# Second operand buffer stored in rows of 272 elements, and transposed probabilities of the first keys placed in the angle table

## The chip, the cores and the metric

The kernel runs on one NeuronCore of a Trainium2 chip. The metric is the device time of one execution in microseconds, the median of several runs. Everything is float32 in memory. The matrix products are made on TensorE from operands that are split in a high and a low part.

## What is computed

Two transformer blocks, one after the other, on one sequence of 256 tokens with 2048 features. The first puts 16 learned tokens in front, so it works on 272.

```python
def reference(x, meta, ...):
    x = first_block(...)      # h = [meta, x]
                              # h += mixer(rmsnorm(h)) @ w_out    attention with a forget gate, and a short convolution
                              # h += (silu(h @ w_gate) * (h @ w_up)) @ w_down
                              # rmsnorm(h)[:, 16:]
    return second_block(x, ...)
                              # q, k, v, u, gates = x @ w_in ; rope ; dilated attention ; pooling
                              # merged @ w_out ; layer_norm
                              # f = square(relu(x @ w_ff1)) @ w_ff2 ; layer_norm(ALPHA * x + f)
```

## The kernel before, in words

Features lie on the 128 partitions and tokens along the free dimension, so a product takes a 128x128 weight tile as the stationary operand and a strip of up to 512 columns of activations as the moving operand. All weights stream from memory once, in units of 128 partitions by 1024 elements (4096 bytes per partition): two contraction tiles (kt) of four output tiles (x). SyncE loads units into `raw` (5 slots), ScalarE rounds each into `w_hi` (L812) and VectorE subtracts it to get `w_lo` (L1203), both with 4 slots. A plan, `make_plan`, writes out the steps: a block of four output tiles runs over all its units, and in each unit over its four tiles. All engines walk the same list of steps and meet in semaphores.

The activations that TensorE reads stand in two buffers, `a_op` and `b_op`. Each has for every contraction tile kt two rows, the high part (index 0) and the low part (index 1):

```python
a_op = sb("a_op", [P, KT, 2, TOK], F32R)        # TOK = 272
b_op = sb("b_op", [P, KT, 2, SEQ + 2], F32R)    # SEQ + 2 = 258
```

So in `a_op` a row has 1088 bytes per partition, and in `b_op` 1032. Stages that read `a_op`: k, q, v, conv, gu (gate and up of the first feed-forward), k2, q2, v2, u, gate, out2, ff2. Stages that read `b_op`: out, down, ba, bp, ff1. Stages alternate so that one buffer is filled while the other is read. `a_op` is read from element 16 on in the stages that leave the 16 learned tokens out; `b_op` from element 0.

In most stages ("pair" columns) `product_step` reads both rows in one instruction, as a pattern of 2 rows by 256 elements. For the even kt of a unit it issues L578, w_hi times both rows (512 columns), and L579, w_lo times the high row (256 columns); for the odd kt L581, w_lo times the high row, and L582, w_hi times both rows. These four instructions are called a quad here: 1536 columns of moving data. There are 1984 quads on `a_op` and 992 on `b_op`: 128 in out, 64 in group 0 of down and 96 in each of its groups 1 to 3, 128 in ba and bp, and 128 in each of groups 1 to 3 of ff1. Group 0 of ff1 ("affine" columns) takes two more columns, the 257th and 258th element of each row, which hold the gain and the bias of the layer norm, and makes three products of 258 columns (L585, L586, L587). The stages k, v and most of conv are also made of such threes.

`b_op` is written by ScalarE (high rows: L905, L942, L973, L1053, L1068, L1085) and VectorE (low rows: L1368, L1427, L1525, L1634, L1660, L1726).

`probs_t2` is used in the attention of the first block alone: eight times, once a head, ScalarE copies the transposed probabilities of keys 256 to 271 into it (L882, 16 partitions by 128 elements) and TensorE reads it (L677). `turn_tab` (512 elements a partition) holds, in its first 272 elements on 8 partitions, the running sum of the forget gates (`csum`, L1294, read at L1296 and L638, all by 88 us), and from 484 us on the tables of sines and cosines of the rotary embedding (`sinr` in elements 256 to 511, `cosr` in 0 to 255).

Buffers are laid out in SBUF in the order of their declaration: `h`, `a_op`, `b_op`, `raw`, `w_hi`, `w_lo`, `q`, `k`, `v`, `ytile`, `probs`, `probs_t`, `probs_t2`, then constants and work buffers. They fill all but about 1.4 KB of a partition.

Of the kernel before, what the change touches and what calls it, by code (L numbers as in the profile page):

```python
# [8 lines left out]
F32R = mybir.dt.float32r  # L9
# [5 lines left out]
P = 128  # L15
D = 2048
KT = D // P
SEQ = 256
META = 16
TOK = META + SEQ  # L20
# [161 lines left out]
def two_blocks(nc, w, tokens, params, consts, mask1, mask2, positions, out):  # L182
# [5 lines left out]
    with ExitStack() as ctx:  # L188
        def sb(name, shape, dt=F32):
            return ctx.enter_context(nc.sbuf_tensor(name, shape, dt))  # L190
# [4 lines left out]

        h = sb("h", [P, KT, TOK])
        a_op = sb("a_op", [P, KT, 2, TOK], F32R)
        b_op = sb("b_op", [P, KT, 2, SEQ + 2], F32R)
        raw = sb("raw", [P, RAW, UNIT])
        w_hi = sb("w_hi", [P, SPLIT, UNIT], F32R)  # L200
        w_lo = sb("w_lo", [P, SPLIT, UNIT], F32R)
# [3 lines left out]
        ytile = sb("ytile", [P, KT, SEQ])  # L205
        probs = sb("probs", [P, 2, SEQ + TOK])
        probs_t = sb("probs_t", [P, 2 * SEQ])
        probs_t2 = sb("probs_t2", [META, P])
        con = sb("con", [P, N_CONST])
        masks = sb("masks", [P, 2 * (P + SEQ)])  # L210
        par = sb("par", [P, N_PARAMS])
# [1 line left out]
        row = sb("row", [P, TOK])  # L213
        shift = sb("shift", [P, SEQ])
        turn_tab = sb("turn_tab", [P, 2 * SEQ])
        cosr, sinr = turn_tab[:, 0:SEQ], turn_tab[:, SEQ:2 * SEQ]
        acc = sb("acc", [P, TOK])
        acc2 = sb("acc2", [P, SEQ])
# [1837 lines left out]
```

## Time and profile before

| | |
|---|---|
| median of 3 runs | 2489.11 us (2488.93 to 2490.05) |
| the profiled execution's own time | 2489.91 us |
| its span, first to last instruction | 2488.1 us |
| TensorE busy with matmuls | 2451.6 us, 99% of the span |
| weight loads on TensorE (beside the matmuls) | 2170.8 us, 87% |
| VectorE, ScalarE, GpSimd busy | 1616.2, 1193.4, 217.2 us (65, 48, 9%) |
| granted TensorE clock, mean | 0.996 of full |
| DMA | 449.60 MB, mean 181 GB/s; the weight queue's packets take 57.0% of 16 engines' span |

The profiled execution took 0.80 us more than the median, and 1.8 us of its time lie outside its span. Durations of matmuls overlap in the profile: an instruction of 512 columns is shown as 390 to 400 ns long while the next one starts about 230 ns after it. What a stage costs is therefore read from the starts of its instructions.

### The profile page before, as it was taken

The numbers are of one execution on the slowest core, as the hardware profiler recorded it, in microseconds if no ns is written. First come the engines' busy times: TensorE is split into PE (matmuls) and PEld (weight loads), VectorE is DVE, ScalarE is ACT, GpSimd is POOL, SyncE is SP. The second block draws the span as 40 slices with busy tenths as digits, with TensorE's granted clock in tenths as the row PEclk, the third lists the DMA queues.
The fourth block names the chain that finished last, engine by engine and source line by source line (L and its number), as shares of the span: only waits on it lengthen the run. The fifth ranks groups of instructions, "written<-read, shape, count | busy, mean of one in ns | idle before, by whom it ended". The sixth has DMA issues, their size and how long they took to land.

```text
span 2488.1 us, 36373 instructions
## 1 busy us (share of the span) xinstructions
PE 2451.6 (99%) x14746; PEld 2170.8 (87%) x14746; DVE 1616.2 (65%) x2466; ACT 1193.4 (48%) x1724; POOL 217.2 (9%) x231
## 2 busy tenths in 40 slices
PE   8999999999999999999999999999999999999997
PEld 8898888888888888888888888888998888888885
DVE  5645577766666665667676756677885665565667
ACT  6444445544444443455554544555454443443544
POOL 0001111000000000001220202033200000000022
PEclk9999999999999999999999999999999999999998
DMA  7554445566665656656555465565565666666563
GB/s 246 171 159 128 124 155 181 183 198 189 191 188 179 196 192 187 187 186 201 186 185 154 143 212 190 182 195 183 162 198 187 187 188 190 188 189 191 181 193 102
DMA packets 125752, 449.60 MB, mean 181 GB/s; under 512 B 13840, under 2 KB 16400, under 8 KB 125584
## 3 DMA queue, kind: packets, MB, share of 16 engines
q1 hardware_dynamic: 125296, 446.91, 57.0%
q8 instruction: 116, 1.90, 0.3%
q14 instruction: 52, 0.43, 0.0%
q10 hardware_dynamic: 288, 0.36, 0.0%
HBM read 445.12 MB, written 2.10 MB: 180 GB/s over the span
## 4 chain that ended last, share of the span: by engine, by line
PE 94%; DVE 3%; ACT 1%; issue 1%; DMA 0%; SPq 0%; POOL 0%; ACTq 0%; DVEq 0%
PE out_bank L582 27%; PE out_bank L578 27%; PE out_bank L581 14%; PE out_bank L579 14%; PE out_bank L585 3%; PE out_bank L586 3%; PE out_bank L587 3%; DVE w_lo L1203 1%; ACT w_hi L812 1%; DMA raw<-in_w_in 0%; PE side_bank L657 0%; PE side_bank L656 0%; PE side_bank L695 0%; PE out_bank L604 0%; PE side_bank L679 0%
## 5 line engine op out<-in xcount | busy, mean ns | idle before, releaser
L1203 DVE TENSOR_TENSOR w_lo<-raw,w_hi 128x1024 fp32r<-128x1024 f32 x839 | 1039.8, 1242 | 634.7 <-ACT w_hi L812 631.5
L812 ACT CAST w_hi<-raw 128x1024 fp32r<-128x1024 f32 x840 | 876.6, 1048 | 958.6 <-PE out_bank L582 873.2
L582 PE MATMUL out_bank<-a_op,w_hi 128*128 128x512 f32 x1984 | 785.1, 396 | 0.0
L578 PE MATMUL out_bank<-a_op,w_hi 128*128 128x512 f32 x1984 | 781.6, 394 | 1.5 <-DVE w_lo L1203 0.8
L581 PE MATMUL out_bank<-a_op,w_lo 128*128 128x256 f32 x1984 | 557.6, 281 | 0.0
L579 PE MATMUL out_bank<-a_op,w_lo 128*128 128x256 f32 x1984 | 550.1, 277 | 0.0
L579 PEld LDWEIGHTS out_bank<-a_op,w_lo 128*128 128x128 f32 x1984 | 372.6, 188 | 83.0
L581 PEld LDWEIGHTS out_bank<-a_op,w_lo 128*128 128x128 f32 x1984 | 371.8, 187 | 83.2
L582 PE MATMUL out_bank<-b_op,w_hi 128*128 128x512 f32 x992 | 392.0, 395 | 0.0
L578 PE MATMUL out_bank<-b_op,w_hi 128*128 128x512 f32 x992 | 391.6, 395 | 0.0
L578 PEld LDWEIGHTS out_bank<-a_op,w_hi 128*128 128x128 f32 x1984 | 373.8, 188 | 4.6 <-DVE w_lo L1203 2.4
L582 PEld LDWEIGHTS out_bank<-a_op,w_hi 128*128 128x128 f32 x1984 | 372.8, 188 | 0.0
L579 PE MATMUL out_bank<-b_op,w_lo 128*128 128x256 f32 x992 | 278.4, 281 | 0.0
L581 PE MATMUL out_bank<-b_op,w_lo 128*128 128x256 f32 x992 | 277.5, 280 | 0.0
L581 PEld LDWEIGHTS out_bank<-b_op,w_lo 128*128 128x128 f32 x992 | 187.7, 189 | 43.5
L579 PEld LDWEIGHTS out_bank<-b_op,w_lo 128*128 128x128 f32 x992 | 186.9, 188 | 44.4
L582 PEld LDWEIGHTS out_bank<-b_op,w_hi 128*128 128x128 f32 x992 | 186.8, 188 | 0.0
L578 PEld LDWEIGHTS out_bank<-b_op,w_hi 128*128 128x128 f32 x992 | 186.7, 188 | 0.0
L1220 DVE TENSOR_TENSOR work<-work,out_bank 128x256 f32<-128x256 f32 x248 | 102.5, 416 | 118.6 <-ACT work L831 117.8
L585 PE MATMUL out_bank<-a_op,w_hi 128*128 128x258 f32 (+1 forms) x504 | 147.4, 292 | 0.1
L586 PE MATMUL out_bank<-a_op,w_hi 128*128 128x258 f32 (+1 forms) x504 | 144.5, 287 | 0.0
L587 PE MATMUL out_bank<-a_op,w_lo 128*128 128x258 f32 (+1 forms) x504 | 144.0, 286 | 0.0
(285 smaller groups left out, 1998.0 us busy)
## 6 DMA issues: line engine op xcount, KB each, us to landing
raw<-in_w_ff SPq DMA_DIRECT2D x256, 512.0 KB, 4.2
raw<-in_w_in SPq DMA_DIRECT2D x223, 512.0 KB, 3.7
raw<-in_w_gu SPq DMA_DIRECT2D x176, 512.0 KB, 4.2
raw<-in_w_down SPq DMA_DIRECT2D x88, 512.0 KB, 4.2
raw<-in_w_out SPq DMA_DIRECT2D x64, 512.0 KB, 4.3
raw<-in_w_ba SPq DMA_DIRECT2D x16, 512.0 KB, 4.2
raw<-in_w_bp SPq DMA_DIRECT2D x16, 512.0 KB, 4.1
out<-h SPq DMA_DIRECT2D x8, 256.0 KB, 2.1
```

Source lines behind the costliest of these rows:

```text
L578: t_.e.matmul(bank[:, :], wh, a_both, start=start, stop=False, skip_group_check=True)
L579: mm = t_.e.matmul(bank[:, 0:SEQ], wl, a_hi, start=False, stop=stop, skip_group_check=True)
L581: t_.e.matmul(bank[:, 0:SEQ], wl, a_hi, start=False, stop=False, skip_group_check=True)
L582: mm = t_.e.matmul(bank[:, :], wh, a_both, start=False, stop=stop, skip_group_check=True)
L585: t_.e.matmul(to, wh, a_hi, start=start, stop=False, skip_group_check=True)
L586: t_.e.matmul(to, wh, a_lo, start=False, stop=False, skip_group_check=True)
L587: mm = t_.e.matmul(to, wl, a_hi, start=False, stop=stop, skip_group_check=True)
L812: a.e.copy(w_hi[:, m % SPLIT, :], raw[:, u % RAW, :]).then_inc(hi_split)
L1203: v_.e.tensor_tensor(w_lo[:, m % SPLIT, :], raw[:, u % RAW, :], w_hi[:, m % SPLIT, :].bitcast(F32), ALU.subtract).then_inc(lo_split)
L1220: v_.e.tensor_tensor(y, y, bank_of(tile)[:, 0:SEQ], ALU.add).then_inc(bank_free)
```

## The change

`b_op` gets rows of 272 elements, so that a row has 1088 bytes and a contraction tile 2176, as in `a_op`; before it was 1032 and 2064. Nothing is written to or read from the elements added, and every instruction takes the same numbers of elements as before. That costs 1792 bytes more per partition. `probs_t2` is no longer a buffer (512 bytes less): it is elements 272 to 399 of `turn_tab` on 16 partitions, behind `csum` and inside the later `sinr`.

```diff
-        b_op = sb("b_op", [P, KT, 2, SEQ + 2], F32R)
+        b_op = sb("b_op", [P, KT, 2, TOK], F32R)
...
-        probs_t2 = sb("probs_t2", [META, P])
...
         turn_tab = sb("turn_tab", [P, 2 * SEQ])
+        probs_t2 = turn_tab[0:META, TOK:TOK + P]
         cosr, sinr = turn_tab[:, 0:SEQ], turn_tab[:, SEQ:2 * SEQ]
```

No engine's list of instructions changes, but for the name of the tile in the 8 copies at L882 and the 8 matmuls at L677. The addresses: `h` and `a_op` stay (`a_op` at 33920, `b_op` at 68736), `raw` to `probs_t` move up by 1792 bytes (`raw` from 101760 to 103552, `w_hi` from 122240 to 124032), and everything from `con` on by 1280. In bytes from a multiple of 64, the start of the high row in `b_op` was 16 x kt and of the low row 16 x kt + 8 (modulo 64); it is now 0 for every row, as in `a_op`.

## Rows read from the trace of the kernel before

**Rows 1.** The page's busy times and the chain that ended last.
```profile
span 2488.1 us, 36373 instructions
PE 2451.6 (99%) x14746; PEld 2170.8 (87%) x14746; DVE 1616.2 (65%) x2466; ACT 1193.4 (48%) x1724; POOL 217.2 (9%) x231
...
PE 94%; DVE 3%; ACT 1%; issue 1%; DMA 0%; SPq 0%; POOL 0%; ACTq 0%; DVEq 0%
```

**Rows 2.** Stretches of gu 3, down 3, ff1 2, ff2 2: busy time (instructions), clock, DMA.
```profile
core 0: us, PE busy (x) PEld busy (x) DVE busy (x) ACT busy (x) POOL busy (x), PEclk, DMA share, GB/s
...
980.00:1113.00 133.00, 133.00 (x769) 116.45 (x768) 81.62 (x117) 63.96 (x91) 0.00 (x0) 1.00 0.61 190
1113.00:1180.00 67.00, 67.00 (x384) 58.48 (x383) 50.16 (x73) 36.45 (x56) 10.40 (x11) 1.00 0.60 193
...
2109.00:2198.00 89.00, 89.00 (x510) 77.71 (x509) 53.00 (x75) 42.07 (x58) 0.00 (x0) 1.00 0.62 187
2199.00:2287.00 88.00, 88.00 (x510) 77.05 (x509) 51.94 (x69) 34.81 (x36) 0.00 (x0) 1.00 0.61 190
```

**Rows 3.** Line L578 by stage on `a_op` (gu 1, gu 3, gate 1, ff2 1): count, duration min/median/max, first and last start.
```profile
L578 PE MATMUL out_bank<-a_op,w_hi x192: 388/390/390, 579.2 to 711.6; 128*128 128x512 f32 x192
L578 PE MATMUL out_bank<-a_op,w_hi x192: 390/390/397, 980.0 to 1112.4; 128*128 128x512 f32 x192
L578 PE MATMUL out_bank<-a_op,w_hi x128: 390/390/400, 1519.9 to 1607.9; 128*128 128x512 f32 x128
L578 PE MATMUL out_bank<-a_op,w_hi x128: 390/390/400, 2020.1 to 2108.2; 128*128 128x512 f32 x128
```

**Rows 4.** Line L578 by stage on `b_op` (down 0, down 1, down 3, ba/bp, ff1 1).
```profile
L578 PE MATMUL out_bank<-b_op,w_hi x64: 387/392/397, 534.5 to 578.5; 128*128 128x512 f32 x64
L578 PE MATMUL out_bank<-b_op,w_hi x96: 387/394/405, 712.3 to 778.9; 128*128 128x512 f32 x96
L578 PE MATMUL out_bank<-b_op,w_hi x96: 387/394/405, 1113.1 to 1179.7; 128*128 128x512 f32 x96
L578 PE MATMUL out_bank<-b_op,w_hi x64: 387/394/405, 1475.0 to 1519.2; 128*128 128x512 f32 x64
L578 PE MATMUL out_bank<-b_op,w_hi x128: 387/394/405, 1930.3 to 2019.4; 128*128 128x512 f32 x128
```

**Rows 5.** Timeline of TensorE in ff1 2: the starts of kt 10, 12, 14 and the next kt 0.
```profile
2122.85 0.40 PE L578 MATMUL out_bank<-b_op,w_hi 128*128 128x512 f32 x1
...
2125.66 0.39 PE L578 MATMUL out_bank<-b_op,w_hi 128*128 128x512 f32 x1
...
2128.43 0.40 PE L578 MATMUL out_bank<-b_op,w_hi 128*128 128x512 f32 x1
...
2131.27 0.40 PE L578 MATMUL out_bank<-b_op,w_hi 128*128 128x512 f32 x1
```

**Rows 6.** Line L578 on `a_op` in q2 and in ff2 0.
```profile
L578 PE MATMUL out_bank<-a_op,w_hi x64: 388/394/399, 1226.0 to 1270.1; 128*128 128x512 f32 x64
L578 PE MATMUL out_bank<-a_op,w_hi x128: 388/390/399, 1840.7 to 1929.6; 128*128 128x512 f32 x128
```

**Rows 7.** Groups of the products of 258 columns on both buffers: busy us, mean ns | idle before.
```profile
L585 PE MATMUL out_bank<-a_op,w_hi 128*128 128x258 f32 x256 | 75.4, 294 | 0.0
L586 PE MATMUL out_bank<-a_op,w_hi 128*128 128x258 f32 x256 | 73.1, 285 | 0.0
L586 PE MATMUL out_bank<-b_op,w_hi 128*128 128x258 f32 x256 | 72.9, 285 | 0.0
L585 PE MATMUL out_bank<-b_op,w_hi 128*128 128x258 f32 x256 | 72.8, 284 | 0.2 <-DVE w_lo L1203 0.2
```

**Rows 8.** Groups of VectorE that write low rows, and the copy and product of `probs_t2` (shown as probs_t).
```profile
L1641 DVE TENSOR_TENSOR a_op<-work,a_op 128x256 fp32r<-128x256 f32 x64 | 25.8, 422 | 0.0
L1427 DVE TENSOR_TENSOR b_op<-work,b_op 128x256 fp32r<-128x256 f32 x44 | 18.4, 419 | 0.0
...
L882 ACT COPY probs_t<-side_bank x8: 249/254/256, 175.2 to 294.1; 16x128 f32<-16x128 f32 x8
```

## Prediction

> **What bounds the kernel now.** I read the page's busy times and its chain first: TensorE is busy with matmuls 99% of the span and holds 94% of the chain that ended last, while the other engines stand at 65, 48 and 9% [rows 1]. Then the busy time in four stretches of the long feed-forward stages: TensorE is busy for the whole of each, at full clock, with VectorE at about 60% and the DMA engines at 0.61 [rows 2]. So nothing feeds TensorE too slowly there. What sets the end is the pace at which TensorE itself goes from one matmul to the next, and only an edit that changes that pace, or makes it wait, can show.
>
> The durations of matmuls don't tell the pace, since they overlap. The starts do. Line L578 starts once in each quad (1536 columns of moving data), so the time from the first to the last start of a stage, over the count less one, is the time of a quad:
>
> - On `a_op` [rows 3]: gu 1 and gu 3 take 132.4 us / 191 = 693.2 ns, gate 1 takes 88.0 / 127 = 692.9 ns, ff2 1 takes 88.1 / 127 = 693.7 ns. Call it 693.3.
> - On `b_op` [rows 4]: down 1 and down 3 take 66.6 / 95 = 701.1 ns, ba and bp 44.2 / 63 = 701.6 ns, ff1 1 takes 89.1 / 127 = 701.6 ns, down 0 takes 44.0 / 63 = 698.4 ns.
>
> The same four instructions with the same widths and the same weight tiles are thus about 8 ns slower a quad when the moving operand comes from `b_op`. Nothing waits in either kind of stage. What differs is where the rows begin. In `a_op` every row begins at a multiple of 64 bytes, and the time is the same in whichever stage. In `b_op` the start moves by 16 bytes with each kt and by 8 more for the low row, and the time moves with it. In ff1 2 the four quads of kt 12 and 13 take 2128.43 - 2125.66 = 2.77 us (693 each), those of kt 10 and 11 take 2.81 us (703) and those of kt 14 and 15 take 2.84 us (710) [rows 5]. A buffer whose pace depends on kt, by up to 17 ns, while the instructions are the same, points to the address of the operand. That is the edit's lever.
>
> **The change part by part.**
>
> *Rows of 272 in `b_op`, the pair products.* No instruction is added, removed or moved. I price 992 quads at the pace of `a_op`, 693.3: 288 in down 1 to 3 x 7.8 ns = 2.2 us; 384 in ff1 1 to 3 x 8.3 = 3.2 us; 128 in ba and bp x 8.3 = 1.1 us; 64 in down 0 x 5.1 = 0.3 us; and 128 in out, a stage with other work between, taken at the same 8.3 as an estimate, 1.1 us. Sum 7.9 us. All of it lies on TensorE's path, at full weight.
>
> `a_op` has a second pace, though. In q2 and in ff2 0 a quad takes 44.1 / 63 and 88.9 / 127 = 700.0 ns, the same instructions from the same aligned rows [rows 6]. There L578 is shown with durations from 388 to 399 ns, where gu 1 has 388 to 390. So aligned rows don't give 693.3 for certain: TensorE has two patterns and can stay in either for a whole stage. If `b_op` takes the slow one, the gain is 288 x 1.1 + 512 x 1.6 + 128 x 1.6 = 1.3 us, less 64 x 1.6 = 0.1 for down 0: 1.2 us. These are the bounds of this term: 1.2 and 7.9 us. Of the `a_op` stages that have little else on TensorE (gu 1 to 3, gate 1, ff2 1 and 2 with 960 quads, against q2 and ff2 0 with 192) five sixths run at the fast pace. Weighted so, the gain is 5/6 x 7.9 + 1/6 x 1.2 = 6.8 us. I take this value.
>
> What limits the trust in it: the high row of `b_op` will begin at 0 modulo 128 and the low row at 64, while `a_op` without its 16 learned tokens has it the other way round (64, then 0). No stage of before runs pairs in that arrangement.
>
> A low row of `b_op` begins 8 bytes past a multiple of 16 now, for every kt alike, and a high row at a multiple of 16. If only those 8 bytes mattered, the price would be the same at each kt, and rows 5 show that it isn't; what they would cost is rival C below. The Trainium skill (SBUF — State Buffer, "Door 1: The DMA port swizzle", the note on SBUF cachelines) says that SBUF has lines of 16 bytes and that each access that crosses to a new line pays a penalty. By that rule it would be just these 8 bytes that cost: 65 lines a low row where aligned ones have 64.
>
> *The products of 258 columns in ff1 0.* Their groups on `b_op` are no slower than on `a_op`: 285 against 285 ns at L586, 284 against 294 at L585 [rows 7]. I take zero, bounded by half the quads' difference, as each such three has half the columns: 256 threes x 4.2 ns = 1.1 us either way.
>
> *Writes to the low rows.* VectorE takes 419 ns into `b_op` and 422 into `a_op` [rows 8]: nothing to gain, and VectorE has room.
>
> *`probs_t2` in `turn_tab`.* Eight copies of 254 ns on ScalarE [rows 8] and eight small products keep their form and place. `csum` and `probs_t2` don't overlap, the sines are written some 180 us after the last of these copies. Zero.
>
> *Everything from `raw` on moved by 1792 bytes.* The distance between the moving operand and the weights changes. But in before this distance already changes with each unit (4352 bytes of operand against 4096 of weights) and the quads of gu 1 stay within 388 to 390 ns in duration and at 693.2 in pace [rows 3]. So I take zero. If the distance did matter, the bound is that of the slow pattern, below.
>
> *What is late next.* With 8 ns less per quad nothing new binds: in gu the same chain of split and load serves the faster pace, without a gap [rows 2].
>
> **Sum.** The profiled execution took 2489.91 us, 0.80 more than the median; I forecast medians. 2489.91 - 0.80 - 6.8 = 2482.3 us.
>
> **The rivals.**
>
> *A: aligned rows alone don't help.* `b_op` settles in the slow pattern, or the arrangement 0/64 is not as good as 64/0, or the pace hangs on something other than the row's start. For it: q2 and ff2 0 at 700.0 ns on rows that all begin at a multiple of 64 [rows 6]. Against: kt 12 reaches 693 with its high row on a multiple of 64, and the dependence on kt. Gain between 0 and 2 us, 2487 to 2489 us.
>
> *B: slower, because the pattern is inherited.* In before, gu 1, gu 3, gate 1 and ff2 1 come straight after a stage on `b_op`, and run fast; q2 and ff2 0 come after k2 (on `a_op`) and after the threes of ff1 0, and run slow. Perhaps the irregular rows of `b_op` shake TensorE out of the slow pattern each time, and once all rows are aligned nothing does: the slow one, once entered, lasts over the stages. Then 960 quads on `a_op` lose 700.0 - 693.3 = 6.7 ns each, 6.4 us, against the 1.2 us that `b_op` still gains: 5.2 us slower, 2494.3 us. It decides once more than 180 of the 960 quads change over (180 x 6.7 = 1.2 us) with `b_op` in the slow pattern too. For it: both patterns last for whole stages. Against: the side work of attention and norms, and each change of buffer, disturb TensorE as well.
>
> *C: only the 8 bytes of the low rows cost.* Each quad reads a low row twice (L578, L582), and a fetch of 4 elements more at 693.3 / 1536 = 0.451 ns a column costs 1.8 ns; 1984 such reads make 3.6 us, 2485.5 us. For it: `b_op` is slower on average by a few ns. Against: kt 12 runs at 693 with the same 8 bytes, and kt 14 at 710 [rows 5]. This is what the cachelines note of the Trainium skill would make of the change; no stage here has a pair with low rows alone shifted.
>
> *D: more than forecast.* All of `b_op` at 693.3 (7.9 us) and the stages now slow turned fast as well: 192 quads in q2 and ff2 0 x 6.7 = 1.3 us, and perhaps 1.5 us in stages that mix both. 10.7 us, 2478.4 us.
>
> **How the numbers follow.** Measuring this kernel can tell 0.2%, 5.0 us, from no change: faster is under 2484.1, slower over 2494.1. Forecast (2480 to 2485 us) 0.42, D 0.08, A 0.32, B 0.08, C 0.06, something not thought of 0.04 (half of it slower). Faster: the forecast's and D's, less a small part of the forecast that ends above 2484.1: 0.47. Slower: 0.08 (part of B stops short of the bound). Same: 0.45. The range has to take in the forecast and A, which with C hold 8 in 10: 2479.5 to 2489.5 us, and with some room for the stages of `a_op` that may change pattern, to 2490. The forecast's own range is 2480 to 2485.
>
> **What would show it.** Right: the starts of L578 in down, ff1, ba and bp give 693 to 696 ns a quad; kt 12 and kt 14 take the same time in ff1 2; the longest duration of L578 on `b_op` falls from 405 to 400 ns or less; gu, gate 1 and ff2 1 stay at 693. A: `b_op` at 700, with durations of L578 up to 399. B: gu or ff2 1 at 700. Wrong altogether if TensorE gains idle time before L578 or if VectorE's writes into `b_op` change by more than some ns.

## The result and the profile after

The changed kernel takes 2495.14 us (median of 10 runs, 2492.68 to 2496.45), the kernel before 2490.28 us in the same comparison (2488.93 to 2492.47). The ratio is 1.0019, 95% interval 1.0011 to 1.0027: 4.9 us slower, against a forecast of 6.8 us faster. The profiled execution took 2496.45 us with a span of 2494.6 us.

The page's busy times and chain, to hold against [rows 1]:

```profile
span 2494.6 us, 36373 instructions
PE 2457.9 (99%) x14746; PEld 2174.6 (87%) x14746; DVE 1615.8 (65%) x2466; ACT 1193.4 (48%) x1724; POOL 217.2 (9%) x231
...
PE 94%; DVE 3%; ACT 1%; issue 1%; DMA 0%; SPq 0%; ACTq 0%; DVEq 0%
```

The same engine bounds the kernel, the other engines did the same work in the same time, and TensorE is busy 6.3 us longer. Its pace by stage, line L578 on `b_op` in down 1, down 3, ba/bp, ff1 1 and ff1 2, to hold against [rows 4] (count, duration min/median/max in ns, first and last start in us):

```profile
L578 PE MATMUL out_bank<-b_op,w_hi x96: 390/398/398, 714.9 to 782.0; 128*128 128x512 f32 x96
L578 PE MATMUL out_bank<-b_op,w_hi x96: 391/398/398, 1116.8 to 1183.9; 128*128 128x512 f32 x96
L578 PE MATMUL out_bank<-b_op,w_hi x64: 390/398/398, 1479.8 to 1524.3; 128*128 128x512 f32 x64
L578 PE MATMUL out_bank<-b_op,w_hi x128: 390/397/398, 1934.9 to 2024.6; 128*128 128x512 f32 x128
L578 PE MATMUL out_bank<-b_op,w_hi x128: 390/397/398, 2114.0 to 2203.8; 128*128 128x512 f32 x128
```

A quad now takes 67.1 / 95 = 706.3, 44.5 / 63 = 706.3 and 89.7 / 127 = 706.3 ns, where before it took 701. The expectations below write 706.7, the pace within a stage: the first unit of a stage, with quads of about 700, is not in it. Neither pace of `a_op` (693.3 and 700.0) has appeared on `b_op`, but a third one. The dependence on kt is gone, as forecast. Four starts of line L578 in ff1 2, for kt 10, 12, 14 and the next kt 0, to hold against [rows 5]:

```profile
2128.14 0.40 PE L578 MATMUL out_bank<-b_op,w_hi 128*128 128x512 f32 x1
...
2130.97 0.40 PE L578 MATMUL out_bank<-b_op,w_hi 128*128 128x512 f32 x1
...
2133.80 0.40 PE L578 MATMUL out_bank<-b_op,w_hi 128*128 128x512 f32 x1
...
2136.62 0.40 PE L578 MATMUL out_bank<-b_op,w_hi 128*128 128x512 f32 x1
```

A unit (four output tiles, so four quads) takes 2.82 or 2.83 us, where before the units took 2.77 to 2.84. Aligned rows made the pace even, at a worse level. On `a_op` (gu 3, q2, ff2 0), to hold against [rows 3] and [rows 6]:

```profile
L578 PE MATMUL out_bank<-a_op,w_hi x192: 390/390/392, 983.7 to 1116.1; 128*128 128x512 f32 x192
L578 PE MATMUL out_bank<-a_op,w_hi x64: 390/390/391, 1230.1 to 1273.8; 128*128 128x512 f32 x64
L578 PE MATMUL out_bank<-a_op,w_hi x128: 389/390/400, 1846.1 to 1934.2; 128*128 128x512 f32 x128
```

gu 3 stays at 132.4 / 191 = 693.2 ns, and q2 and ff2 0 went from 700.0 to the fast pace (43.7 / 63 and 88.1 / 127, 693.7 ns). So the change costs 992 x 5.3 = 5.3 us on `b_op`, and 192 quads of `a_op` take 1.2 us less: 0.8 in ff2 0 and 0.4 in q2. The 0.4 us can't be put down to the new rows, since q2 is fast with the old ones too (old_rows below). That makes 4.1 of the 4.9 us. The spans of the two profiled executions differ by 6.5 us, because in the one of after TensorE's granted clock was lower in q and in u. Stretches 61 to 90, 90 to 112, 1316 to 1376 and 86 to 91 us, before and then after (the number ahead of the DMA share is the mean granted clock):

```profile
61.00:90.00 29.00, 26.27 (x156) 22.74 (x155) 18.97 (x40) 16.78 (x25) 0.00 (x0) 1.00 0.47 146
90.00:112.00 22.00, 22.00 (x131) 19.36 (x130) 12.13 (x15) 9.52 (x13) 0.00 (x0) 1.00 0.63 191
1316.00:1376.00 60.00, 58.01 (x339) 50.13 (x338) 45.23 (x102) 28.92 (x47) 9.57 (x16) 1.00 0.50 154
...
86.00:91.00 5.00, 3.28 (x19) 2.91 (x20) 4.83 (x11) 1.39 (x3) 0.00 (x0) 1.00 0.23 51
```

```profile
61.00:90.00 29.00, 26.27 (x150) 22.67 (x149) 19.11 (x39) 16.54 (x25) 0.00 (x0) 0.97 0.48 146
90.00:112.00 22.00, 22.00 (x122) 19.27 (x121) 10.41 (x13) 8.38 (x10) 0.00 (x0) 0.96 0.60 188
1316.00:1376.00 60.00, 58.14 (x331) 50.38 (x330) 42.51 (x95) 28.99 (x48) 6.61 (x12) 0.97 0.49 151
...
86.00:91.00 5.00, 3.45 (x14) 3.00 (x15) 4.83 (x11) 1.39 (x3) 0.00 (x0) 0.73 0.22 66
```

In q the fall stands at a pause of TensorE, which is busy for 3.3 to 3.5 of these 5 us in both executions; the kernel before kept its full clock through it. Such a dip is not tied to the new rows: the profiled execution of old_rows has 0.97 and 0.96 in the first two of these stretches, and 1.00 in the third. The dips cost 3.0 us here, 1.7 in q and 1.3 in u, by the starts of line L578.

### The profile page after: what moved, and what is told of

Read it like the earlier page. It is cut to its first block, busy times and chain, and to the rows that moved or that the text cites. A ratio compares the mean times of both kernels' runs of the same rounds, so it can differ in the third digit from the quotient of the medians.

```text
span 2494.6 us, 36373 instructions
## 1 busy us (share of the span) xinstructions
PE 2457.9 (99%) x14746; PEld 2174.6 (87%) x14746; DVE 1615.8 (65%) x2466; ACT 1193.4 (48%) x1724; POOL 217.2 (9%) x231
## 4 chain that ended last, share of the span: by engine, by line
PE 94%; DVE 3%; ACT 1%; issue 1%; DMA 0%; SPq 0%; ACTq 0%; DVEq 0%
PE out_bank L578 27%; PE out_bank L582 27%; PE out_bank L581 14%; PE out_bank L579 14%; PE out_bank L585 3%; PE out_bank L586 3%; PE out_bank L587 3%; DVE w_lo L1203 1%; ACT w_hi L812 0%; DMA raw<-in_w_in 0%; PE side_bank L657 0%; PE side_bank L656 0%; PE side_bank L695 0%; PE out_bank L604 0%; PE side_bank L679 0%
## 5 line engine op out<-in xcount | busy, mean ns | idle before, releaser
L582 PE MATMUL out_bank<-a_op,w_hi 128*128 128x512 f32 x1984 | 787.2, 397 | 0.0
L578 PE MATMUL out_bank<-a_op,w_hi 128*128 128x512 f32 x1984 | 782.6, 394 | 1.6 <-DVE w_lo L1203 0.9
L578 PE MATMUL out_bank<-b_op,w_hi 128*128 128x512 f32 x992 | 394.4, 398 | 0.0
L582 PE MATMUL out_bank<-b_op,w_hi 128*128 128x512 f32 x992 | 389.9, 393 | 0.0
L578 PEld LDWEIGHTS out_bank<-a_op,w_hi 128*128 128x128 f32 x1984 | 374.2, 189 | 4.6 <-DVE w_lo L1203 2.5
L582 PEld LDWEIGHTS out_bank<-a_op,w_hi 128*128 128x128 f32 x1984 | 373.3, 188 | 0.0
L579 PE MATMUL out_bank<-b_op,w_lo 128*128 128x256 f32 x992 | 282.5, 285 | 0.0
L581 PE MATMUL out_bank<-b_op,w_lo 128*128 128x256 f32 x992 | 279.8, 282 | 0.0
L582 PEld LDWEIGHTS out_bank<-b_op,w_hi 128*128 128x128 f32 x992 | 187.5, 189 | 0.0
L578 PEld LDWEIGHTS out_bank<-b_op,w_hi 128*128 128x128 f32 x992 | 186.3, 188 | 0.0
L585 PE MATMUL out_bank<-a_op,w_hi 128*128 128x258 f32 (+1 forms) x504 | 147.5, 293 | 0.6 <-DVE a_op L1208 0.5
L586 PE MATMUL out_bank<-a_op,w_hi 128*128 128x258 f32 (+1 forms) x504 | 144.5, 287 | 0.0
```

What stands on the lines that cost most here:

```text
L578: t_.e.matmul(bank[:, :], wh, a_both, start=start, stop=False, skip_group_check=True)
L579: mm = t_.e.matmul(bank[:, 0:SEQ], wl, a_hi, start=False, stop=stop, skip_group_check=True)
L581: t_.e.matmul(bank[:, 0:SEQ], wl, a_hi, start=False, stop=False, skip_group_check=True)
L582: mm = t_.e.matmul(bank[:, :], wh, a_both, start=False, stop=stop, skip_group_check=True)
L585: t_.e.matmul(to, wh, a_hi, start=start, stop=False, skip_group_check=True)
L586: t_.e.matmul(to, wh, a_lo, start=False, stop=False, skip_group_check=True)
```

## Experiments

The theory after the result was that the pace depends on where the rows of the moving operand begin modulo 128 (theory P). The first rivals were that it depends on their place relative to the weights (R), or on something other than addresses (Q). In all kernels below each instruction is as in the changed one, but for the two nudges; only places in SBUF differ. Each diff is against the changed kernel, and that of before_w_128 against the kernel before. Each kernel has one profiled execution, so a pace of a stage is read from one execution, while the times are medians of 2 to 11. For reference, with places modulo 256 and the weights' start taken off: the high row at an even kt stands at 64 in `a_op`, before and after, and at 0 in `b_op` after. This is called rel from the second set on. At odd kt it is 128 more.

**Old rows in the new places** (label old_rows)

```diff
-        b_op = sb("b_op", [P, KT, 2, TOK], F32R)
+        b_op = sb("b_op", [P, KT, 2, SEQ + 2], F32R); pad1 = sb("pad1", [P, KT * 28])
```

> The changed kernel with b_op back in rows of 258 elements and 1792 bytes of padding behind it, so that every other buffer stands exactly where the change put it, probs_t2 inside turn_tab too. If the rows of b_op are the whole cause: b_op back at about 701 ns a quad, 5.3 us less than the changed kernel, the time of before (2490). If the moved buffers or the place of probs_t2 cost something by themselves: it stays above before by that, up to 2495.

Measured: 2489.82 us, ratio to before 0.9999 (0.9989 to 1.0008). Line L578 in gu 3, down 3, q2 and ff2 0:

```profile
L578 PE MATMUL out_bank<-a_op,w_hi x192: 390/390/397, 981.7 to 1114.2; 128*128 128x512 f32 x192
L578 PE MATMUL out_bank<-b_op,w_hi x96: 387/394/405, 1114.9 to 1181.4; 128*128 128x512 f32 x96
L578 PE MATMUL out_bank<-a_op,w_hi x64: 390/390/390, 1227.7 to 1271.3; 128*128 128x512 f32 x64
L578 PE MATMUL out_bank<-a_op,w_hi x128: 388/390/399, 1841.7 to 1930.6; 128*128 128x512 f32 x128
```

`b_op` is back at 66.5 / 95 = 700 ns with the scattered durations of before. The loss comes from the rows of `b_op`. The moved buffers, and `probs_t2` in `turn_tab`, cost nothing that the interval of 0.1% would show. ff2 0 is back at 88.9 / 127 = 700.0 ns as well, but q2 is not: it takes 43.6 us for 63 quads, the fast pace, where before it took 44.1, though all that TensorE reads there has the same places modulo 256 and the same widths. So a stage can change from one pace to the other without any of these edits.

**`b_op` 64 bytes further** (label b_at_64)

```diff
+        pad0 = sb("pad0", [P, 16])
         b_op = sb("b_op", [P, KT, 2, TOK], F32R)
+        pad1 = sb("pad1", [P, 16])
```

> The changed kernel with 64 bytes of padding ahead of b_op and 64 behind it: high rows of b_op begin at 64 modulo 128 and low rows at 0, as the rows of a_op do in the pair stages; everything else stays where it is modulo 128. Theory P (the pace is set by where the moving rows begin modulo 128, and 64 then 0 is the good order, 0 then 64 the bad one): quads on b_op go from 706.7 to 693.3 ns, 992 x 13.4 ns = 13.3 us less than the changed kernel (about 2482), so 8 us less than before. Rival Q (the stages on b_op are slower for another reason, such as the engines that write or the stage's own waits): 706.7 stays, 2495. Theory P but with the slow pattern of q2 in some stages: 693 to 700, 2482 to 2488.

Measured: 2497.78 us, ratio 1.0025 (1.0015 to 1.0034). A miss for P and for Q. gu 3 and down 3:

```profile
L578 PE MATMUL out_bank<-a_op,w_hi x192: 392/394/395, 985.2 to 1118.9; 128*128 128x512 f32 x192
L578 PE MATMUL out_bank<-b_op,w_hi x96: 392/394/395, 1119.6 to 1186.1; 128*128 128x512 f32 x96
```

`b_op` did get better, 66.5 / 95 = 700.0 ns, but `a_op`, which was not touched, went from 693.3 to 133.7 / 191 = 700.0. What had moved for `a_op` was the weights, by 128 bytes.

**Only what lies behind `b_op` 64 bytes further, and only the split weights** (labels weights_at_64, only_w_64)

```diff
         b_op = sb("b_op", [P, KT, 2, TOK], F32R)
+        pad1 = sb("pad1", [P, 16])                       # weights_at_64
...
+        pad0 = sb("pad0", [P, 16])                       # only_w_64
         w_hi = sb("w_hi", [P, SPLIT, UNIT], F32R)
         w_lo = sb("w_lo", [P, SPLIT, UNIT], F32R)
+        pad1 = sb("pad1", [P, 16])                       # only_w_64
```

> The changed kernel with 64 bytes of padding behind b_op only: a_op and b_op stay, the weights (raw, w_hi, w_lo) and all behind them now begin at 64 modulo 128. Theory P (place of the moving rows alone): nothing changes, a_op at 693.3 and b_op at 706.7 ns a quad, 2495 us. Rival R (the place of the moving rows relative to the weights counts, both being read at once): the roles swap, a_op goes to 706.7 (1984 x 13.4 = 26.6 us more) and b_op to 693.3 (13.3 us less), 2508 us.

> The changed kernel with 64 bytes between raw and w_hi and 64 behind w_lo: only the split weights, which TensorE loads, stand 64 bytes further modulo 128; raw, the work buffers and all others keep their places. If the pace hangs on the moving rows against the loaded weights: as in weights_at_64, a_op at 706.7 (rel 0) and b_op at 700.0 (rel 192), near 2507 us. If on another buffer that moved along in weights_at_64 (raw, the work buffers): as the changed kernel, 693.3 and 706.7, 2495 us.

Measured: 2507.41 us (ratio 1.0065, 1.0047 to 1.0084) and 2506.65 us (1.0067, 1.0044 to 1.0090). gu 3 and down 3 in weights_at_64:

```profile
L578 PE MATMUL out_bank<-a_op,w_hi x192: 390/397/398, 986.1 to 1121.1; 128*128 128x512 f32 x192
L578 PE MATMUL out_bank<-b_op,w_hi x96: 392/394/400, 1121.8 to 1188.3; 128*128 128x512 f32 x96
```

and in only_w_64:

```profile
L578 PE MATMUL out_bank<-a_op,w_hi x192: 390/397/398, 986.0 to 1121.0; 128*128 128x512 f32 x192
L578 PE MATMUL out_bank<-b_op,w_hi x96: 392/394/400, 1121.7 to 1188.2; 128*128 128x512 f32 x96
```

Neither operand moved, and the paces changed on both: `a_op` to 135.0 / 191 = 706.8 ns, `b_op` to 700.0. P is out. The second run leaves `raw` in place, and the work buffers at their places modulo 128 (they move by 128, where weights_at_64 moved them by 64), and does the same, so it is the place of the moving rows against the weights that TensorE loads that counts. R had `b_op` at 693.3; it is 700.0, at rel 192 where `a_op` used to have rel 64.

**`b_op` and the weights moved together** (label both_at_64)

```diff
+        pad0 = sb("pad0", [P, 16])
         b_op = sb("b_op", [P, KT, 2, TOK], F32R)
```

> The changed kernel with 64 bytes of padding ahead of b_op only: b_op and the weights both begin at 64 modulo 128, a_op stays. Theory P: a_op 693.3, b_op 693.3, about 2482 us. Rival R (relative place): b_op keeps 706.7 since it moved along with the weights, and a_op goes to 706.7 as well, 2495 + 26.6 = 2522 us.

Measured: 2515.57 us, ratio 1.0098 (1.0080 to 1.0116). gu 3 and down 3:

```profile
L578 PE MATMUL out_bank<-a_op,w_hi x192: 397/397/398, 990.1 to 1125.0; 128*128 128x512 f32 x192
L578 PE MATMUL out_bank<-b_op,w_hi x96: 397/397/398, 1125.7 to 1192.9; 128*128 128x512 f32 x96
```

As R says: `b_op` keeps its bad pace when it moves along with the weights, and `a_op` gets it too. The forecast of 2522 was too high: it took 13.4 ns more for each of 1984 quads. The 1152 quads of gu 1 to 3, q2, gate 1 and ff2 0 to 2 did lose 13.3, and gu 0 12.3, but k2 and ff2 3 lost 8.2, out2 7.6, v2 5.8 and group 0 of gate 3.1, where the quad in the middle took 704 ns already.

**`b_op` at rel 64 with the weights kept modulo 256** (label b_at_64_w_kept)

```diff
+        pad0 = sb("pad0", [P, 16])
         b_op = sb("b_op", [P, KT, 2, TOK], F32R)
+        tiny = sb("tiny", [P, 3, 16])
...
-        tiny = sb("tiny", [P, 3, 16])
```

> The changed kernel with 64 bytes ahead of b_op and the small buffer tiny moved behind it (192 bytes), so that the weights move by 256 in all. Write rel for the start of the high row at an even kt less the start of the weights, modulo 256. The runs so far had rel 64 (a_op before and after: mostly 693.3 ns a quad), rel 0 (b_op of the changed kernel, both buffers of both_at_64, a_op of weights_at_64: 706.7) and rel 192 (both buffers of b_at_64, b_op of weights_at_64: 700.0). Here both buffers have rel 64. Theory G (rel alone sets the pace): 693.3 on both, 992 x 13.4 = 13.3 us less than the changed kernel, about 2482. Rival H (with all rows alike the slow pattern is entered and kept, which is why b_at_64 ran at 700.0 everywhere): 700.0 on both, like b_at_64, about 2497. Between: some stages at each.

Measured: 2486.98 us, ratio 0.9987 (0.9978 to 0.9996), the first layout that beats the kernel before. gu 3, down 3, ff1 2 and ff2 2:

```profile
L578 PE MATMUL out_bank<-a_op,w_hi x192: 390/390/390, 977.5 to 1110.0; 128*128 128x512 f32 x192
L578 PE MATMUL out_bank<-b_op,w_hi x96: 390/390/390, 1110.7 to 1176.5; 128*128 128x512 f32 x96
L578 PE MATMUL out_bank<-b_op,w_hi x128: 388/394/399, 2106.9 to 2195.8; 128*128 128x512 f32 x128
L578 PE MATMUL out_bank<-a_op,w_hi x128: 388/394/399, 2196.5 to 2285.4; 128*128 128x512 f32 x128
```

Both G and H are half right. In gu 1 to 3 and in down all quads run at 693, `b_op` included (65.8 / 95 = 693). From ba on, behind the stages with much other work on TensorE, ba, bp, gate 1, ff2 0 to 2 and ff1 1 to 3 all run at 88.9 / 127 = 700.0, `a_op` included, which before ran fast in gate 1 and ff2 2. So rel 64 has two patterns. The pace from the starts tells them apart; durations do so less surely (388/390/399 in ff2 0 of before is slow, 389/390/400 in ff2 0 of after is fast).

The starts also show where TensorE changes from one to the other. In ff2 3 of this kernel, the quads ahead of two small products of the layer norm and those behind them:

```profile
L578 PE MATMUL out_bank<-a_op,w_hi x40: 388/394/399, 2375.7 to 2403.0; 128*128 128x512 f32 x40
...
2404.44 0.59 PE L735 MATMUL side_bank<-acc,ones 128*128 128x256 f32 x2
...
L578 PE MATMUL out_bank<-a_op,w_hi x57: 390/390/390, 2409.7 to 2448.6; 128*128 128x512 f32 x57
```

They take 27.3 / 39 = 700 and 38.9 / 56 = 695 ns (693.4 by the starts to the hundredth of a us). In the profiles of the seven kernels with `a_op` at rel 64 no two neighbouring units on `a_op` that ran at the paces 693 and 700 differed in it: between a fast unit and a slow one there always stands a unit lengthened by something else, or another stage. q2 takes over the pace at which k2 ends, 700 in before and 693 in old_rows.

**`b_op` at rel 128** (label b_at_128_w_kept) and **the kernel before with the weights 128 bytes further** (label before_w_128)

```diff
+        pad0 = sb("pad0", [P, 32])                                # b_at_128_w_kept
         b_op = sb("b_op", [P, KT, 2, TOK], F32R)
+        gms = sb("gms", [P, KT, 2])                               # and taken out below
...
         b_op = sb("b_op", [P, KT, 2, SEQ + 2], F32R)
+        pad1 = sb("pad1", [P, 32])                                # before_w_128
```

> As the run beside it, but with 128 bytes ahead of b_op and gms behind it: b_op has rel 128, a_op keeps rel 64. Not seen so far. Theory G: b_op takes some fixed pace of its own; since even and odd kt merely change roles between rel 0 and rel 128, 706.7 is the guess (2495 us), 693 to 700 possible (2482 to 2489). a_op stays at 693.3 in gu 1 to 3 by both theories.

> The kernel before with 128 bytes behind b_op: its irregular rows of 258 stay, but a_op gets rel 192 where it had 64. Theory G: a_op goes from 693.3 to 700.0 in gu 1 to 3, gate 1 and ff2 1 and 2: 960 x 6.7 = 6.4 us more than before, about 2496. Rival H (irregular rows shake TensorE into the fast pattern, whatever rel is): a_op stays at 693.3 in these stages, 2490.

Measured: 2495.35 us (ratio 1.0022, 1.0012 to 1.0032) and 2500.34 us (1.0037, 1.0023 to 1.0052). gu 3 and down 3 of b_at_128_w_kept:

```profile
L578 PE MATMUL out_bank<-a_op,w_hi x192: 390/390/399, 981.8 to 1114.3; 128*128 128x512 f32 x192
L578 PE MATMUL out_bank<-b_op,w_hi x96: 392/395/397, 1115.0 to 1182.1; 128*128 128x512 f32 x96
```

and gu 3 and ff2 2 of before_w_128:

```profile
L578 PE MATMUL out_bank<-a_op,w_hi x192: 392/394/400, 984.8 to 1118.5; 128*128 128x512 f32 x192
L578 PE MATMUL out_bank<-a_op,w_hi x128: 392/394/395, 2208.8 to 2297.7; 128*128 128x512 f32 x128
```

Rel 128 gives 67.1 / 95 = 706.3 ns, as guessed. In before_w_128 `a_op` runs at 700.0 with rel 192 although `b_op` keeps its irregular rows: at rel 192 no fast pattern was seen, with irregular rows or without. The stages of the estimate lost 6.3 us, as forecast. The time rose by 9.7 us: gu 0, out2, ff2 3, k2 and v2 lost 1.7 us more, and the stages on `b_op`, whose rows had moved against the weights as well, about 0.8 us. For the rest, 0.9 us, no stage is known.

**Other places** (labels rel_32, rel_96), as b_at_64_w_kept, with `pad1` of 8 elements behind `tiny`, or `ln_tiny` and 16 elements in place of `tiny`.

> b_at_64_w_kept with the weights 32 bytes further, so that both buffers have rel 32. Not seen with rows all alike; in the kernel before, quads at kt 2 (high row at rel 32, the odd kt's 16 bytes beyond) took 699 ns. If the pace falls in steps of 6.7 ns between 0 (706.7) and 64 (693.3 or 700.0): 700.0, near 2495. The quads of before were never under 691, so no gain is expected.

> The same with the weights 32 bytes nearer, both buffers at rel 96. In the kernel before kt 6 took 705 and kt 14 took 710 ns. If that belongs to the place of the high row: 706.7 or more on both, 2976 quads x 13.4 ns above 693.3, about 2520 us.

Measured: 2515.25 us (ratio 1.0098, 1.0080 to 1.0117) and 2498.63 us (1.0031, 1.0019 to 1.0044). gu 3, first rel_32, then rel_96:

```profile
L578 PE MATMUL out_bank<-a_op,w_hi x192: 397/397/397, 988.8 to 1123.8; 128*128 128x512 f32 x192
```

```profile
L578 PE MATMUL out_bank<-a_op,w_hi x192: 395/395/395, 984.0 to 1117.7; 128*128 128x512 f32 x192
```

Both guesses missed, rel_32 to the slow side and rel_96 to the fast, and for one reason: I carried the paces of kt 2, 6 and 14 over from the kernel before, where the low row and the odd kt stand elsewhere. Rel 32 is as bad as 0, and 96 as 192.

| rel of the high row, even kt | ns a quad | seen on |
|---|---|---|
| 0 | 706 to 707 | `b_op` after; both buffers in both_at_64; `a_op` in weights_at_64, only_w_64 |
| 32 | 707 | both in rel_32 |
| 64 | 693.3 or 700.0 | `a_op` before and after; both in b_at_64_w_kept |
| 96 | 700.0 | both in rel_96 |
| 128 | 706 | `b_op` in b_at_128_w_kept |
| 192 | 700.0 | both in b_at_64; `b_op` in weights_at_64, only_w_64; `a_op` in before_w_128 |

Rel 0 and rel 192 were each seen with the weights at two different places modulo 256, and had the same pace at both.

**A nudge at the start of a stage** (labels nudge_shifted, nudge_plain). On top of b_at_64_w_kept, 17 matmuls more, each written to a bank and overwritten there by the product that follows:

```diff
+                        if start and tile is first_tile[blk.stage, blk.group] and blk in late:
+                            t_.e.matmul(bank[:, 0:240], wh, a_hi[:, 16:256], start=True, stop=True, skip_group_check=True)
```

with `late` the blocks of pair columns from ba on; nudge_plain reads `a_hi[:, 0:240]`.

> b_at_64_w_kept with one matmul of 240 columns more at the start of 17 stages from ba on, written to the stage's first bank and overwritten by the product that follows; its moving operand begins 64 bytes later, at rel 128. Theory H+ (rel 64 has two patterns; a stage keeps the one it is in, and reading once from rows in the arrangement 0/128 throws TensorE into the fast one, as down, ba, bp and ff1 do for the stages behind them in the changed kernel): the stages from ba to ff1 3, some 1024 quads at 700.0, go to 693.3: 6.9 us less, 17 x 0.12 = 2.0 us more, 2482 us. Rival: one matmul is too little, or only what stands just before a stall matters: 2.0 us more, 2489.

> The same with the added matmul's operand at rel 64 like all others. Theory H+ in its strict form (the odd address does it): stays at 700.0, 2489 us. Rival (any break in the rhythm can do it): some or all stages go to 693.3, 2482 to 2486.

Measured: 2484.07 us (ratio 0.9972, 0.9961 to 0.9982) and 2484.16 us (0.9974, 0.9964 to 0.9984). The statement of L578 stands at L582 in these two. gate 1, ff1 1 and ff1 2 of nudge_shifted:

```profile
L582 PE MATMUL out_bank<-a_op,w_hi x128: 390/390/396, 1520.1 to 1608.2; 128*128 128x512 f32 x128
L582 PE MATMUL out_bank<-b_op,w_hi x128: 388/390/399, 1930.5 to 2019.4; 128*128 128x512 f32 x128
L582 PE MATMUL out_bank<-b_op,w_hi x128: 390/390/396, 2109.1 to 2197.2; 128*128 128x512 f32 x128
```

and of nudge_plain:

```profile
L582 PE MATMUL out_bank<-a_op,w_hi x128: 388/389/399, 1516.7 to 1605.6; 128*128 128x512 f32 x128
L582 PE MATMUL out_bank<-b_op,w_hi x128: 390/390/392, 1927.1 to 2015.2; 128*128 128x512 f32 x128
L582 PE MATMUL out_bank<-b_op,w_hi x128: 390/390/392, 2104.8 to 2192.9; 128*128 128x512 f32 x128
```

Each nudge kernel has slow stages left, and they aren't the same ones: nudge_shifted has gate 1 at 88.1 / 127 = 693.7 and ff1 1 at 700.0, nudge_plain the other way round. So the pattern of a stage turned with the nudges in, the odd address isn't needed for it (the strict form of H+ fell), and it doesn't turn each time. The times agree: of the 16 runs with nudges 15 lie below 2485.4 us, and all 11 of b_at_64_w_kept above 2485.8, with the kernel before at 2490.98 beside the first and 2490.60 beside the second. Whether the added matmul does it, or only the 0.1 us by which it moves what follows, isn't separated; q2 above changed without one. Both kernels come out about 0.27% under the kernel before and 11 us under the changed one. That a timing as fine as this survives other edits of the program is not shown.

## Why the prediction was wrong

- *What bounds the kernel, and the lever.* Right. TensorE's pace from matmul to matmul decides, the rows of `b_op` set it, and nothing else in the change counts (old_rows).
- *"I price 992 quads at the pace of `a_op`, 693.3."* This is the step that failed, with its bounds of 1.2 and 7.9 us: both were paces of `a_op`, so both belonged to one arrangement. The text itself said that the new arrangement (0, then 64) was run by no stage of before, and then gave that doubt no price. The runs showed 706.3 ns in its place (706.7 behind a stage's first unit), 5.3 ns a quad worse than the irregular rows: 5.3 us lost on `b_op`, not 1.2 to 7.9 us gained. "Aligned" was the wrong notion: all rows that begin at a multiple of 64 gave 693.3, 700.0 or 706.7, by their place against the weights. The nearest rows of the trace were those of kt 0 and kt 8, whose high rows had rel 0 and 128, and not those of `a_op`. They took 697 to 702 and 702 to 705 ns, which speaks against a gain but doesn't give 706.7 either; their low rows stood 8 bytes behind the high ones modulo 256, not 64.
- *"and the time moves with it"*. The reading of rows 5 was incomplete, and so was "the time is the same in whichever stage" for `a_op`, which q2 and ff2 0 contradict. The same kt has two paces at the same addresses. In ff1 2 of before, the starts of kt 4 and kt 6 in the first block of four output tiles, then in the second:

```profile
2114.43 0.40 PE L578 MATMUL out_bank<-b_op,w_hi 128*128 128x512 f32 x1
...
2117.21 0.40 PE L578 MATMUL out_bank<-b_op,w_hi 128*128 128x512 f32 x1
...
2136.87 0.39 PE L578 MATMUL out_bank<-b_op,w_hi 128*128 128x512 f32 x1
...
2139.69 0.40 PE L578 MATMUL out_bank<-b_op,w_hi 128*128 128x512 f32 x1
```

kt 4 and 5 take 2.78 us in one and 2.82 us in the other, 695 against 705 ns a quad; in down they take 2.78. So the pace depends on the address and on the rhythm in which TensorE arrives there, with irregular rows too, and a price can't be read off one kt.

- *The moved weights.* Zero was right for this change, since 1792 is 7 x 256, and 256 is also the step (4352 less 4096) by which I argued that distance doesn't count. As a rule it was wrong: a shift of the weights by 64 in only_w_64 costs 11 to 12 us over the changed kernel.
- *The two patterns.* That TensorE has two paces at the same addresses and keeps one was right, and b_at_64_w_kept and q2 in old_rows show it. The weight of 5/6 taken from it was worth nothing, since `b_op` entered neither.
- *Rival A* came nearest to the cause, with "the arrangement 0/64 is not as good as 64/0", but let the gain fall to 0 at worst, though nothing bounded it there.
- *Rival B* named the side on which it came out, 5.2 us slower against 4.9 measured, but by another way: `a_op` did not lose its pace, it ran faster on 192 quads. Its mechanism exists (the kept slow pattern of b_at_64_w_kept) and had no part in the loss.
- *Rival C*, the 8 bytes of the low rows, would have made the change faster by 3.6 us. With all rows at multiples of 16 the quads on `b_op` went from 701 to 706 ns, so these bytes did not set the pace; that they cost nothing beside it isn't shown, as no run moves the low rows alone. The note on cachelines in the Trainium skill (SBUF — State Buffer, "Door 1: The DMA port swizzle") says that an access that crosses to a new line of 16 bytes pays a penalty. The pace measured here went the other way.
- *The signs.* Three of the signs set down for a right forecast came true in the slower kernel: kt 12 and kt 14 take the same time, the longest duration fell from 405 to 398 ns, and gu, gate 1 and ff2 1 stayed at 693. They show even rows and not fast ones; only the pace itself could tell.
- *The small terms.* The products of 258 columns, the writes of VectorE and the eight copies at L882 were priced at nothing, and stayed within a few ns an instruction (L585 on `b_op` at 286 and L586 at 283 ns, L1427 at 418, L882 at 254).
- *Odds.* 0.08 for slower was too little for a case whose price I could not read anywhere in the trace. With a doubt like that a bound on the other side, the worst pace seen (710 ns at kt 14), was to be had: 992 x 9 = 9 us slower.

## What to carry to other kernels

When one engine is busy all the time, read its pace from the starts of its instructions, stage by stage, and compare stages with the same instructions: a few ns apiece, times thousands, were the whole game here. If a pace depends on addresses, being aligned is not enough. Two operands that are read at the same time have a place relative to each other, and every buffer declared between them sets it; a sweep of small paddings finds the good ones. A term with no row of its own needs a bound on both sides.

## What the runs showed of the hardware

- The pace of back-to-back matmuls depends on the place in SBUF of the moving rows against the weights being loaded, in the table above: 693.3 to 706.7 ns for 1536 columns, 2% between best and worst. Moving `w_hi` and `w_lo` by 64 bytes against both operands took `a_op` from 693.3 to 706.8 and `b_op` from 706.3 to 700.0. Why the place counts is not shown. Which of the split rows matters, high or low, the distance between them, and `w_hi` moved without `w_lo` weren't tried.
- At one and the same placement TensorE kept either of two rhythms (693.3 or 700.0 ns) over hundreds of microseconds and several stages. In the profiles it changed only across a unit that other work had lengthened, or between stages: in ff2 3 of b_at_64_w_kept two small products stood between 700 and 693.
- The mean granted clock of the stretches in q and in u was 0.96 or 0.97 in the profiled execution of after and 1.00 in that of before, and old_rows has it low in q alone. In q it fell at the pause near 86 us (0.73 over 5 us). It is worth 3.0 us of the difference between the two spans.
